# Three-block float32 network on one core: convolutions that read PSUM banks, and three small steps of the delta rule placed elsewhere

## The chip, the cores and the metric

The kernel runs on one core of one Trainium2 chip. The metric is the device time in microseconds (us) of one execution of the whole program. Engines are named as the profile names them: PE is TensorE (matmuls), ACT ScalarE, DVE VectorE, POOL GpSimd, SP SyncE, which here only issues DMAs.

## The reference

512 positions of width 1024, float32, go through two "hybrid" layers and then one further layer (sparse attention, a recurrent unit and a feed-forward part), which the change does not touch. A hybrid layer, cut to what the change touches:

```python
def hybrid_layer(x, ...):
    h = rms_norm(x, norm_g)
    proj = jnp.einsum('btd,de->bte', h, w_in)
    (qa, ka, va, za, ba, aa, ub, zb, qc, kc, vc, zc, iq, ik, iw, gates) = split_columns(proj)
    ya = deltanet_branch(qa, ka, va, za, ba, aa, conv_w, a_log, dt_bias, dn_onorm)
    ...
    merged = jnp.sum(gate * projected, axis=2).astype(w_out.dtype)
    return x + jnp.einsum('btd,de->bte', merged, w_out).astype(x.dtype)

def deltanet_branch(qa, ka, va, za, ba, aa, conv_w, a_log, dt_bias, o_norm):
    qkv = jax.nn.silu(causal_depthwise_conv(jnp.concatenate([qa, ka, va], axis=-1), conv_w))
    q, k, v = jnp.split(qkv, 3, axis=-1)
    q = l2_normalize(q.reshape(b, t, DN_HEADS, DN_DK))
    k = l2_normalize(k.reshape(b, t, DN_HEADS, DN_DK))
    beta = jax.nn.sigmoid(ba.astype(jnp.float32))
    g = -jnp.exp(a_log) * jax.nn.softplus(aa + dt_bias)
    o = chunk_gated_delta_rule(q, k, v, beta, g)
    o = rms_norm(o, o_norm) * jax.nn.silu(za.reshape(b, t, DN_HEADS, DN_DV))
```

The convolution has four taps over time, per channel. There are four heads of width 128 for each of q, k and v, so twelve groups of 128 channels.

## The kernel before

**Products.** Channels lie in the partitions, the 512 positions in the free dimension. Every weight matrix is cut into "units" of 128x1024 values (303 in all, in the fixed order of `plan()`). To get float32 accuracy, weights and inputs are split into a high and a low part, and a product of 128x128 weights with a 128x512 input is three matmuls (`prod3`): high by high, high by low, low by high. A tile of 128 output channels is one unit: eight such products, 24 matmuls, into one PSUM bank. Each unit goes through a ring of three buffers: SP loads it to `st`, ACT rounds it to `wh` (128x1024), POOL computes `wl` = `st` - `wh` (two pieces of 128x512), PE uses it. ACT may round unit u only when PE is done with unit u-3 (`ahead`, called by `take`), SP may load unit u only when POOL is done with u-3.

**Order.** Each engine runs its own program in order; semaphores join them. A main stage is a generator, and side stages are other generators advanced beside it at fixed rates by `weave` (0.81 steps of `delta` per main step in the stage `proj`; a main step is half a tile). What is left of a side when the main stage ends runs after it, with nothing beside it. A layer goes:

- `norm`: the layer's norm and four gate tiles.
- `front1`: the small tile (beta, decay, index weights), then twelve tiles q, k, v of the delta rule, into banks 4 to 7 in turn. Convolution c: ACT copies the bank to `pad[c % 2]` behind three zeros, writes the first tap to `cv` (a `tmp` buffer) with a second read of the bank, and so frees the bank; DVE adds the other three taps from shifted parts of `pad` (each waits for the one before); ACT computes the tanh; DVE multiplies (silu) into `qf`, `kf` or `vf`. `small(1)`, inside convolution 1, computes the decay's softplus in partitions 32 to 35: Abs, Exp, Ln and an Exp of `a_log` on ACT, three DVE instructions, the last a scan into `L.rw`. SP then copies that row (`rows`).
- `proj` beside `delta` and `select`: three index tiles (two queries, one key; each is copied, swapped by DMAs and rotated on DVE), eight rows for attention and twenty gate tiles. `delta` begins with the head norms: ACT squares eight tiles (`dn_sq`), PE sums them over partitions (`sums`, four matmuls each for q and k), ACT takes the reciprocal root (`rnorm`: Ln and Exp), PE spreads it over the partitions (`spread`, four matmuls into banks 4 to 7), DVE multiplies. Then a transpose of `L.rw` (`tp`), sums of the decay (`gl`), products and inverses per chunk, and four chunks in sequence, whose outputs ACT copies to `L.yA`. It ends with the output norm: four squares, `sums`, `rnorm`, `spread`, and four DVE multiplications (`on_row`). `select` chooses the keys by rounds of maxima on DVE.
- `front3` beside `sparse`: four units of values (`v`), gates, pooling. After the selection and `on_row`, SP loads queries, keys and stored gates; `sparse` is the attention.
- the merge and the output projection.

Helpers record the operations, so most lines of the profile are a helper's: L442 is a matmul, L431 a copy on ACT, L428 another activation, L376, L382, L386 DVE or POOL elementwise operations (L386 the multiply-add `scalar_tensor_tensor`), L371 a DMA. Tiles tell the place: `wl<-st,wh` is POOL's split, `tmp<-pad,col,tmp` a convolution tap, `bank<-E,cst` and `bank<-R,cst` the sums and spreads of the norms.

Of the kernel before, what the change touches and what calls it, by code (L numbers as in the profile page):

```python
# [274 lines left out]
class Nothing:  # L275
# [18 lines left out]
    "act_rows": "pl_p qk_sq qk_r q2_sq q2_r k2_sq k2_r conv_th zc_a pl_a ga_a gelu_a rec_a",  # L294
# [215 lines left out]
def build(nc, units, consts, tabA, tabB, cols, poolw, lruw, phi1, phi2, x_in, x_out, cpack, apack, bpack):  # L510
# [9 lines left out]
    def done(*key):  # L520
        return at("unit", place[key])
# [30 lines left out]
    for l in range(2):  # L552
# [20 lines left out]
        L.Y, L.E, L.R = [[sb(f"{n}{e}{l}", [128, T], stack=dtmp) for e in range(2)] for n in "YER"]  # L573
# [154 lines left out]
    def tensor_program(e):  # L728
# [89 lines left out]

        def delta(l):
            L, aa4 = layer[l], layer[l].aa4  # L820
            def sums(b, name, *key):

                o = bank(b, name, *key)
                for c, q in enumerate(Q4):
                    pe.wait_ge(*at(f"{name}_sq", *key, c))
                    t = pe.mm(o[q, :], ones[:, 0:32], (L.aa4k if key[1:] == (1,) else aa4)[c][:], True, True)
                t.then_inc(*sig(f"{name}_mm", *key))

            def spread(src, name, *key):

                pe.wait_ge(*at(f"{name}_r", *key))
                for c, q in enumerate(Q4):
                    t = pe.mm(bank(4 + c, f"{name}_row", *key, c), first[q, :], src[q, :], True, True)
                t.then_inc(*sig(f"{name}_up", *key))

            yield
            sums(4, "dn", l, 0)
            yield
            sums(5, "dn", l, 1)
# [8 lines left out]
            for i in range(4):  # L848
                t = pe.tr(o[:, sq4(i)], L.rw[:, sq4(i)], ident)
# [81 lines left out]
            yield  # L931
            sums(4, "on", l)
            yield
            yield
            spread(aa4[0], "on", l)
            yield

# [16 lines left out]
        def front3(l):  # L954
            L, g = layer[l], f"n{l}"
            for b in range(4):
                bank(b, "vs", l, b)
            for j in range(4):
                n = take("v", l, j)
                for b in range(4):  # L960
                    for kk in range(2):
# [7 lines left out]
                t.then_inc(*sig("unit", n))  # L969
                yield  # L970
# [322 lines left out]
    def scalar_program(e):  # L1293
# [72 lines left out]
        def front1(l):  # L1366
# [4 lines left out]
            z1, z2 = L.E  # L1371

            def small(c):
                if c == 0:
                    ac.wait_ge(*done("small", l))
                    ac.act(L.scs[R0, :], banks[4][R0, :], ACT.Tanh, 0.5).then_inc(*sig("small_a", l, 0))
                if c == 1:
# [76 lines left out]
        def delta(l):  # L1454
# [63 lines left out]
            for c in range(4):  # L1518
                ac.act(aa4[c][:], L.yA[:, c, :], ACT.Square).then_inc(*sig("on_sq", l, c))
# [1492 lines left out]
```

## Time and profile before

| | |
|---|---|
| time, median of 3 runs | 2039.75 us (2035.28 to 2040.04) |
| the profiled execution: its own time | 2041.28 us |
| the profiled execution: span | 2039.5 us |
| PE busy | 1991.6 us (98% of the span), 9420 matmuls |
| PE weight loads busy | 1568.8 us (77%) |
| DVE busy | 1067.9 us (52%) |
| ACT busy | 914.9 us (45%) |
| POOL busy | 874.6 us (43%) |
| DMA | 228.53 MB, mean 112 GB/s |
| mean granted TensorE clock | 0.994 of full speed |

The span is that of one profiled execution, from first to last instruction; the time beside it is the device time of the same execution. Busy shares are means over many stages. A matmul of 128x512 is shown with about 0.39 us, though in an unbroken row the next one begins 0.23 us after it: matmuls overlap, and a busy PE can still be held up for a part of each of these intervals. So the starts of matmuls in the timeline say more than the busy share. Idle time of another engine costs nothing by itself.

### The profile page before, as it was taken

How to read it: one execution, taken by the hardware profiler on the slowest of the kernel's cores; microseconds unless marked ns; L12 is line 12 of the kernel's file. 1: busy time of each engine (PE TensorE's matmuls, PEld its weight loads, DVE VectorE, ACT ScalarE, POOL GpSimd, SP SyncE). 2: the span in 40 equal slices, each digit the busy share in tenths (PEclk: the TensorE clock that was granted, in tenths of full speed). 3: DMA queues.
4: the chain of work that ended last, by engine and by line, in shares of the span. 5: the costliest groups of instructions: out<-in, count | busy, mean ns of one | idle time of the engine just before them, and what ended most of it. 6: DMA issues, size and time to landing. Idle time of an engine off the chain costs nothing.

```text
span 2039.5 us, 24488 instructions
## 1 busy us (share of the span) xinstructions
PE 1991.6 (98%) x9420; PEld 1568.8 (77%) x9420; DVE 1067.9 (52%) x1877; ACT 914.9 (45%) x1414; POOL 874.6 (43%) x646
## 2 busy tenths in 40 slices
PE   8999999999999999999999999999999999999999
PEld 6767778777788768787877788676777887888887
DVE  6756845645746658655464747677344256201210
ACT  5555543334345455443334345677555444312321
POOL 5444432434355445431434455455222345444443
PEclk9999999999999999999999999999999999999999
DMA  5234442323534244532423545322111332332232
GB/s 190 97 114 125 139 134 89 136 83 109 185 107 150 87 122 129 154 104 71 151 79 127 178 155 157 132 71 83 53 52 42 108 105 87 103 98 96 96 111 75
DMA packets 90917, 228.53 MB, mean 112 GB/s; under 512 B 25929, under 2 KB 29001, under 8 KB 89489
## 3 DMA queue, kind: packets, MB, share of 16 engines
q1 hardware_dynamic: 89360, 223.82, 33.4%
q10 hardware_dynamic: 1440, 3.15, 0.4%
q8 instruction: 75, 1.23, 0.2%
q14 instruction: 42, 0.34, 0.1%
HBM read 195.06 MB, written 24.64 MB: 108 GB/s over the span
## 4 chain that ended last, share of the span: by engine, by line
PE 73%; DVE 14%; ACT 6%; DMA 3%; issue 2%; SPq 2%; POOL 1%; ACTq 0%; DVEq 0%
PE bank L442 71%; DVE tmp L386 4%; PE bank L445 2%; SPq L371 2%; ACT tmp L428 1%; ACT wh L431 1%; DVE kv L376 1%; DVE E L376 1%; DVE lt L386 1%; POOL wl L376 1%; DVE tmp L376 1%; DMA gt<-gates 1%; DMA pad<-tmp 1%; ACT pad L431 1%; DVE scs L401 1%
## 5 line engine op out<-in xcount | busy, mean ns | idle before, releaser
L376 POOL TENSOR_TENSOR wl<-st,wh 128x512 fp32r<-128x512 f32 x606 | 826.5, 1386 | 1082.7 <-ACT wh L431 1082.6
L442 PE MATMUL bank<-hh,wh 128*128 128x512 f32 x1632 | 664.5, 407 | 18.8 <-POOL wl L376 15.2
L442 PE MATMUL bank<-hl,wh 128*128 128x512 f32 x1632 | 638.6, 391 | 0.0
L442 PE MATMUL bank<-hh,wl 128*128 128x512 f32 x1632 | 638.6, 391 | 0.0
L431 ACT ACTIVATE wh<-st 128x1024 fp32r<-128x1024 f32 x303 | 318.1, 1050 | 235.6 <-PE bank L442 197.5
L442 PEld LDWEIGHTS bank<-hh,wh 128*128 128x128 f32 x1632 | 307.7, 189 | 122.1 <-issue 28.2
L442 PEld LDWEIGHTS bank<-hl,wh 128*128 128x128 f32 x1632 | 308.0, 189 | 66.9 <-issue 6.9
L442 PEld LDWEIGHTS bank<-hh,wl 128*128 128x128 f32 x1632 | 307.7, 189 | 66.1
L376 DVE TENSOR_TENSOR xt<-xt,bank 128x512 f32<-128x512 f32 x40 | 27.4, 687 | 235.7 <-PE bank L442 235.7
L386 DVE SCALAR_TENSOR_TENSOR tmp<-pad,col,tmp 128x512 f32<-128x512 f32 x80 | 81.7, 1022 | 38.9 <-ACT tmp L428 36.9
L442 PE MATMUL bank<-fh,wh 128*128 128x512 f32 x256 | 99.6, 389 | 0.0
L442 PE MATMUL bank<-fl,wh 128*128 128x512 f32 x256 | 99.6, 389 | 0.0
L442 PE MATMUL bank<-fh,wl 128*128 128x512 f32 x256 | 99.6, 389 | 0.0
L428 ACT ACTIVATE tmp<-bank 128x512 f32<-128x512 f32 x62 | 36.9, 596 | 125.6 <-PE bank L442 118.3
L376 DVE TENSOR_TENSOR tmp<-tmp 128x512 f32<-128x512 f32 x32 | 24.6, 770 | 106.4 <-ACT tmp L428 106.3
L442 PE MATMUL bank<-yh,wh 128*128 128x512 f32 x192 | 79.7, 415 | 0.3 <-DVE yl L376 0.3
L428 ACT ACTIVATE tmp<-bank,hb 128x512 f32<-128x512 f32 x40 | 27.6, 689 | 108.3 <-PE bank L442 94.4
L442 PE MATMUL bank<-yh,wl 128*128 128x512 f32 x192 | 75.0, 391 | 0.0
L442 PE MATMUL bank<-yl,wh 128*128 128x512 f32 x192 | 74.8, 390 | 0.0
L428 ACT ACTIVATE tmp<-tmp 128x512 f32<-128x512 f32 x46 | 29.1, 632 | 74.3 <-DVE tmp L386 73.8
L404 DVE CUSTOM_DVE_ANT_0 Ln<-bank,cau 128x128 f32<-128x128 f32 (+3 forms) x64 | 28.9, 489 | 58.0 <-PE bank L442 57.9
L428 ACT ACTIVATE Ln<-Ln,stc 128x128 f32<-128x128 f32 (+3 forms) x64 | 35.5, 556 | 48.9 <-DVE stc L404 48.8
(340 smaller groups left out, 3000.3 us busy)
## 6 DMA issues: line engine op xcount, KB each, us to landing
st<-units SPq DMA_DIRECT2D x303, 512.0 KB, 3.5
gates<-tmp SPq DMA_DIRECT2D x48, 256.0 KB, 2.5
gt<-gates SPq DMA_DIRECT2D x48, 256.0 KB, 3.7
pad<-tmp SPq DMA_DIRECT2D x32, 128.0 KB, 4.6
qk<-tmp SPq DMA_DIRECT2D x16, 256.0 KB, 4.2
x_scratch<-xt SPq DMA_DIRECT2D x2, 2048.0 KB, 8.6
xt<-x_scratch SPq DMA_DIRECT2D x2, 2048.0 KB, 9.1
ph<-phi SPq DMA_DIRECT2D x8, 512.0 KB, 4.5
```

The source lines that it names most:

```text
L371: return NOTHING if self.e is None else self.e.dma_start(out, in_)
L376: return NOTHING if self.e is None else self.e.tensor_tensor(out, a, b, op)
L386: return NOTHING if self.e is None else self.e.scalar_tensor_tensor(out=out, in0=a, scalar=s, in1=b, op0=op0, op1=op1)
L401: return NOTHING if self.e is None else self.e.match_replace(out, vals, a, v)
L404: return NOTHING if self.e is None else self.e.tensor_tensor_reduce(out, a, b, scale, init, ALU.add, red, acc)
L428: return self.e.activation(out, a, func, scale=scale, **kw)
L431: return NOTHING if self.e is None else self.e.activation(out, a, ACT.Copy)
L442: return NOTHING if self.e is None else self.e.matmul(out, lhsT, rhs, start=start, stop=stop, skip_group_check=share)
L445: return NOTHING if self.e is None else self.e.transpose(out, a, ident)
```

## The change

1. **Convolutions.** ACT no longer copies the bank to `pad`. It writes the first tap; DVE adds taps 1 to 3 from the bank itself, each to the columns from its shift on (511, 510 and 509 columns), and the third of them frees the bank. ACT rounds the next unit (`take`) between its first tap and its tanh, while DVE works.
2. **Softplus of the decay.** Its four activations move from convolution 1 to the step of `delta` behind the two `rnorm` of the head norms, its three DVE instructions to just ahead of DVE's multiplication of k, and the copy of the row on SP to the eighth step of `delta`. Its tiles are `L.Y` and not `L.E`.
3. **Squares of the head norms.** Each is computed in convolution c + 4, behind its tanh. PE's two `sums` stand in one step, with one wait each.
4. **Output norm.** Each chunk of `yA` is squared right behind its copy, into the joined tile `L.ER` (E and R of before). `sums` comes behind the first unit of values, `rnorm` in ACT's second step of values, `spread` behind the third unit, and DVE's four multiplications behind all of the selection. Banks 0 to 3 are taken one by one in the first unit of values.
5. The transpose `tp` takes 96 partitions instead of 128.

The core of the diff:

```diff
@@ PE, front3 @@
+                    if j == 0:
+                        bank(b, "vs", l, b)
...
+                if j == 0:
+                    pe.wait_ge(*at("on_sq", l, 3))
+                    sums(4, L.aa4, "on", l)
+                if j == 2:
+                    spread(L.aa4[0], "on", l)
@@ PE, delta @@
-            sums(4, "dn", l, 0)
-            yield
-            sums(5, "dn", l, 1)
+            pe.wait_ge(*at("dn_sq", l, 0, 3))
+            sums(4, aa4, "dn", l, 0)
+            pe.wait_ge(*at("dn_sq", l, 1, 3))
+            sums(5, L.aa4k, "dn", l, 1)
+            yield
...
-                t = pe.tr(o[:, sq4(i)], L.rw[:, sq4(i)], ident)
+                t = pe.tr(o[:, 128 * i:128 * i + 96], L.rw[0:96, sq4(i)], ident[0:96, 0:96])
@@ ACT, front1 @@
-                ac.cp(pad[c % 2][:, 3:3 + T], banks[b][:])
-                ac.act(cv[:], banks[b][:], ACT.Identity, K(f"conv{l}", 4 * c + 3), 0.0).then_inc(*sig(f"free{b}", "conv", l, c))
-                small(c)
-                ac.wait_ge(*at("conv_v", l, c, 3))
+                ac.act(cv[:], banks[b][:], ACT.Identity, K(f"conv{l}", 4 * c + 3), 0.0).then_inc(*sig("conv_0", l, c))
...
+                if c < 11:
+                    take("p", l, 128 * (c + 1))
+                ac.wait_ge(*at(f"free{b}", "conv", l, c))
                 ac.act(th[:], cv[:], ACT.Tanh, 0.5).then_inc(*sig("conv_th", l, c))
+                if c >= 4:
+                    f, h = c // 4 - 1, c % 4
+                    ac.wait_ge(*at("conv_v", l, c - 4, 4))
+                    ac.act((L.aa4, L.aa4k)[f][h][:], (L.qf, L.kf)[f][:, h, :], ACT.Square, 0.5).then_inc(*sig("dn_sq", l, f, h))
@@ ACT, end of delta @@
+                ac.wait_ge(*at(f"free{5 + n % 2}", "yA", l, n))
+                ac.act(L.ER[:, :, sq4(n)], L.yA[:, :, sq4(n)], ACT.Square).then_inc(*sig("on_sq", l, n))
@@ DVE, front1 @@
-                dv.wait_ge(*at(f"free{b}", "conv", l, c))
+                dv.wait_ge(*at("conv_0", l, c))
                 for i in range(1, 4):
...
-                    dv.stt(cv[:], pad[c % 2][:, 3 - i:3 - i + T], K(f"conv{l}", 4 * c + 3 - i), cv[:], ALU.mult, ALU.add).then_inc(*sig("conv_v", l, c, i))
+                    t = dv.stt(cv[:, i:T], banks[b][:, 0:T - i], K(f"conv{l}", 4 * c + 3 - i), cv[:, i:T], ALU.mult, ALU.add)
@@ SP, delta @@
-            yield from idle(8 + 2)
+            yield from idle(7)
+            sp.wait_ge(*at("small_v", l, 4))
+            sp.dma(L.rw[R3, :], L.rw[R1, :]).then_inc(*dma("rows", l))
+            yield from idle(3)
```

Where instructions move, at the three places that the prediction speaks of:

ACT, one convolution of `front1` (c = 5), before; the pair of rows from bank is the copy and the first tap, the last row the tanh:

```order
L431 ACTIVATE wh<-st 128x1024 [waits s_st0]
L431 ACTIVATE pad<-bank 128x512 [waits s_unit]
L428 ACTIVATE tmp<-bank,col 128x512
L428 ACTIVATE tmp<-tmp 128x512 [waits s_dve_rows]
L431 ACTIVATE wh<-st 128x1024 [waits s_st1]
```

and now (c = 7), where `ER<-qf` is a square of the head norms:

```order
L428 ACTIVATE tmp<-bank,col 128x512 [waits s_dve_rows,s_unit]
L431 ACTIVATE wh<-st 128x1024 [waits s_st0]
L428 ACTIVATE tmp<-tmp 128x512 [waits s_free4]
L428 ACTIVATE ER<-qf 128x512
L428 ACTIVATE tmp<-bank,col 128x512 [waits s_dve_rows,s_unit]
```

The rounding of a unit stood between the tanh and the next first tap; it now stands between the first tap and the tanh.

ACT in the index stage of `proj`, before, from the copy of the second index tile on; each pair `E<-bank,cst`, `E<-E` is one `rnorm`:

```order
L431 ACTIVATE tmp<-bank 128x512 [waits s_unit]
L420 ACT_TABLE_LOAD [waits s_pe_heads]
L428 ACTIVATE E<-bank,cst 128x512
L428 ACTIVATE E<-E 128x512 [waits s_free4]
L431 ACTIVATE wh<-st 128x1024 [waits s_st0]
L428 ACTIVATE E<-bank,cst 128x512 [waits s_pe_heads]
L428 ACTIVATE E<-E 128x512 [waits s_free5]
```

and now, the rows on 4 partitions being the softplus:

```order
L431 ACTIVATE tmp<-bank 128x512 [waits s_unit]
L420 ACT_TABLE_LOAD [waits s_pe_heads]
L428 ACTIVATE ER<-bank,cst 128x512
L428 ACTIVATE ER<-ER 128x512 [waits s_free4]
L428 ACTIVATE ER<-bank,cst 128x512 [waits s_pe_heads]
L428 ACTIVATE ER<-ER 128x512 [waits s_free5]
L428 ACTIVATE Y<-Y 4x512 [waits s_dve_small]
L428 ACTIVATE Y<-Y 4x512 [waits s_act_small] x2
L428 ACTIVATE colx<-col 4x1
L431 ACTIVATE wh<-st 128x1024 [waits s_st0]
```

The rounding of the weights (of gate tile 4) has moved behind the second `rnorm` and the softplus.

PE at the end of `delta`, before, where `ki,qi` is the last product of the selection and `wh,hh` the first of the values:

```order
L442 MATMUL bank<-ki,qi 128x512 [waits s_free3]
L442 MATMUL bank<-E,cst 32x512 [waits s_act_heads] x2
L442 MATMUL bank<-R,cst 32x512 [waits s_act_heads] x2
L442 MATMUL bank<-E,cst 128x512 [waits s_free4,s_act_heads]
L442 MATMUL bank<-E,cst 128x512 [waits s_free5]
L442 MATMUL bank<-E,cst 128x512 [waits s_free6]
L442 MATMUL bank<-E,cst 128x512
L442 MATMUL bank<-wh,hh 128x512 [waits s_free3,s_free2,s_lo,s_free1,s_free0]
```

and now:

```order
L442 MATMUL bank<-ki,qi 128x512 [waits s_free3]
L442 MATMUL bank<-wh,hh 128x512 [waits s_free0,s_lo]
L442 MATMUL bank<-wh,hl 128x512
L442 MATMUL bank<-wl,hh 128x512
```

The values follow the selection's product at once; the four sums stand a unit of 24 matmuls later, the four matmuls of the spread 48 further ones behind them.

## Rows read from the trace of the kernel before

**Rows 1.** Waits of TensorE, whole span: engine, line, waited for; us in total, times, longest.
```profile
PE bank L442 <- POOL wl L376: 18.1, 25, 2.9
PE bank L442 <- ACT E L428: 7.5, 4, 2.7
```

**Rows 2.** Timeline of PE, layer 0, convolution stage: start us, us, operation.
```profile
43.97 0.39 PE L442 MATMUL bank<-hh,wh 128*128 128x512 f32 x1
...
63.01 0.39 PE L442 MATMUL bank<-hh,wh 128*128 128x512 f32 x1
...
65.59 0.50 PE L442 MATMUL bank<-hh,wh 128*128 128x512 f32 x1 [1.74 <-POOL wl L376]
...
120.48 0.50 PE L442 MATMUL bank<-hh,wh 128*128 128x512 f32 x1 [0.28 <-POOL wl L376]
```

**Rows 3.** Timeline of DVE and ACT, one convolution of layer 0.
```profile
70.37 3.28 DVE L386 SCALAR_TENSOR_TENSOR tmp<-pad,col,tmp 128x512 f32<-128x512 f32 x3 [1.32 <-ACT tmp L428]
...
73.69 0.63 ACT L428 ACTIVATE tmp<-tmp 128x512 f32<-128x512 f32 x1 [3.35 <-DVE tmp L386]
74.23 1.04 ACT L431 ACTIVATE wh<-st 128x1024 fp32r<-128x1024 f32 x1
75.18 0.58 ACT L431 ACTIVATE pad<-bank 128x512 f32<-128x512 f32 x1
75.65 0.68 ACT L428 ACTIVATE tmp<-bank,col 128x512 f32<-128x512 f32 x1
```

**Rows 4.** Timeline of PE, layer 0, sums and spread of the head norms.
```profile
126.96 0.50 PE L442 MATMUL bank<-hh,wh 128*128 128x512 f32 x1
...
129.91 1.06 PE L442 MATMUL bank<-aT,cst 128*32 128x512 f32 x8
...
130.90 0.50 PE L442 MATMUL bank<-hh,wh 128*128 128x512 f32 x1
...
135.92 0.50 PE L442 MATMUL bank<-hh,wh 128*128 128x512 f32 x1
```

**Rows 5.** Timeline of PE, layer 1, the same two ends of the stage.
```profile
659.03 0.39 PE L442 MATMUL bank<-hh,wh 128*128 128x512 f32 x1
...
730.90 0.50 PE L442 MATMUL bank<-hh,wh 128*128 128x512 f32 x1
```

**Rows 6.** Timeline of DVE and POOL: multiply-adds that read a bank.
```profile
138.80 2.48 DVE L386 SCALAR_TENSOR_TENSOR qf<-qf,bank 128x512 f32<-128x512 f32 x4
...
360.40 1.60 DVE L386 SCALAR_TENSOR_TENSOR scs<-bank,wi,scs 128x512 f32<-128x512 f32 x2 [3.08 <-ACT bank L428]
...
140.59 2.55 POOL L376 TENSOR_TENSOR wl<-st,wh 128x512 fp32r<-128x512 f32 x2 [3.78 <-ACT wh L431]
```

**Rows 7.** Timeline of PE: end of the delta rule, layer 0, and one product of layer 1.
```profile
358.43 1.52 PE L442 MATMUL bank<-E,cst 128*32 128x512 f32 x4
...
364.78 0.50 PE L442 MATMUL bank<-wh,hh 128*128 128x512 f32 x1
...
963.00 0.63 PE L442 MATMUL bank<-wh,hl 128*128 128x512 f32 x1
```

**Rows 8.** Timelines of ACT, DVE and PE: softplus' steps, and the index stage.
```profile
55.72 1.29 ACT L428 ACTIVATE E<-E 4x512 f32<-4x512 f32 x2
...
61.57 1.21 DVE L395 TENSOR_TENSOR_SCAN rw<-cst,E 4x512 f32<-4x512 f32 x1
...
133.19 1.04 ACT L431 ACTIVATE wh<-st 128x1024 fp32r<-128x1024 f32 x1
...
143.47 0.69 DVE L376 TENSOR_TENSOR ki<-tmp,tabs 128x512 f32<-128x512 f32 x1 [2.19 <-DMA tmp<-tmp]
...
149.09 0.60 PE L445 MATMUL bank<-cst,rw 128*128 128x128 f32 x4
```

**Rows 9.** Timelines of SP and PE: loads after the selection, first product with the loaded keys.
```profile
390.14 0.33 SPq L371 DMA_DIRECT2D pw<-poolw  x1
...
425.66 0.38 PE L442 MATMUL bank<-ks,qs 128*128 128x128 f32 x2
```

More of the change, by code:

```diff
@@ L572, in build @@
         L.XT0 = sb(f"XT0{l}", [128, 4, 4, 128], stack=dtmp)
-        L.Y, L.E, L.R = [[sb(f"{n}{e}{l}", [128, T], stack=dtmp) for e in range(2)] for n in "YER"]
+        L.Y = [sb(f"Y{e}{l}", [128, T], stack=dtmp) for e in range(2)]
+        L.ER = sb(f"ER{l}", [128, 4, T], stack=dtmp)
+        L.E, L.R = [L.ER[:, e, :] for e in range(2)], [L.ER[:, 2 + e, :] for e in range(2)]
         kv = sb(f"kv{l}", [128, 4, T], stack=dtmp)
@@ L817, in proj, with sums, spread @@
             yield from lagged(jobs())
+        def sums(b, x, name, *key):
+            o = bank(b, name, *key)
+            for c, q in enumerate(Q4):
+                t = pe.mm(o[q, :], ones[:, 0:32], x[c][:], True, True)
+            t.then_inc(*sig(f"{name}_mm", *key))
+        def spread(src, name, *key):
+            pe.wait_ge(*at(f"{name}_r", *key))
+            for c, q in enumerate(Q4):
+                t = pe.mm(bank(4 + c, f"{name}_row", *key, c), first[q, :], src[q, :], True, True)
+            t.then_inc(*sig(f"{name}_up", *key))
         def delta(l):
             L, aa4 = layer[l], layer[l].aa4
[L821 to L834, printed above, removed]
             yield
-            sums(4, "dn", l, 0)
+            pe.wait_ge(*at("dn_sq", l, 0, 3))
+            sums(4, aa4, "dn", l, 0)
+            pe.wait_ge(*at("dn_sq", l, 1, 3))
+            sums(5, L.aa4k, "dn", l, 1)
             yield
-            sums(5, "dn", l, 1)
             yield
@@ L1456, in delta @@
             ac.wait_ge(*at("hb2", l))
-            for f in range(2):
-                for c in range(4):
-                    ac.wait_ge(*at("conv_v", l, 4 * f + c, 4))
-                    ac.act((aa4, L.aa4k)[f][c][:], (L.qf, L.kf)[f][:, c, :], ACT.Square, 0.5).then_inc(*sig("dn_sq", l, f, c))
-                yield
+            yield
+            yield
             for f in range(2):
@@ L2170, in delta @@
                 yield
-            yield
-            yield
-            yield
-            dv.wait_ge(*at("on_up", l))
-            dv.wait_ge(*at("hn", l))
-            for c in range(4):
-                dv.stt(L.yA[:, c, :], L.yA[:, c, :], colx[:, 1:2], banks[4 + c][:], ALU.mult, ALU.mult).then_inc(*sig(f"free{4 + c}", "on_row", l, c))
-            yield
         def select(l):
@@ L2219, in front3 @@
             L = layer[l]
-            yield from idle(4)
+            yield from idle(3)
+            dv.wait_ge(*at("on_up", l))
+            dv.wait_ge(*at("hn", l))
+            for c in range(4):
+                dv.stt(L.yA[:, c, :], L.yA[:, c, :], colx[:, 1:2], banks[4 + c][:], ALU.mult, ALU.mult).then_inc(*sig(f"free{4 + c}", "on_row", l, c))
+            yield
             for c in range(4):
@@ L2791, in delta @@
             L = layer[l]
-            yield from idle(8 + 2)
+            yield from idle(7)
+            sp.wait_ge(*at("small_v", l, 4))
+            sp.dma(L.rw[R3, :], L.rw[R1, :]).then_inc(*dma("rows", l))
+            yield from idle(3)
             for f in range(2):
```

82 lines of the change are left out of this document (29 added, 53 removed).

## The prediction, made before the changed kernel ran

> **What bounds the kernel now.** I read the busy table first: PE is busy for 1991.6 of 2039.5 us. The other engines are near half, so only time in which PE stands still, or works slower than it can, is to be won. The list of PE's waits says where [rows 1]: the largest are 18.1 us in 25 waits for POOL's low halves of weights, and 7.5 us in 4 waits for ACT's work on tile E, which are the squares and roots of the norms. These are the two places that the change works on. The timelines give their true size, since a modelled matmul covers part of a gap.
>
> In an unbroken row of tiles the k-steps of three matmuls begin 0.68 us apart: 28 steps lie between 43.97 and 63.01 [rows 2]. A tile of eight takes 5.44 us. From the fourth convolution on a tile takes longer: the one that could begin at 63.69 (63.01 + 0.68) begins at 65.59, and nine tiles later, at 120.48, PE has spent 54.9 us, 6.1 each.
>
> The loop that sets this is one convolution [rows 3]. DVE's three taps run from 70.37 for 3.28 us, the tanh begins at 73.69, the rounding of a unit at 74.23, the copy to `pad` at 75.18, the first tap at 75.65, and the next three taps can begin at about 76.37: 6.0 us round, all in series. The rounding of weights sits in it, so POOL and PE go at this pace.
>
> **Part 1, convolutions, softplus and squares: the stage up to the head norms' first spread.** The new loop from the end of a tile: first tap 0.62, three taps, tanh 0.63, for c from 4 a square of 0.6, and about 0.15 of handovers. The rounding lies beside the taps. No row shows this bank-reading tap. The nearest from below are four independent bank-reading multiply-adds in 2.48 us, 0.62 each; from above two dependent ones in 1.60, 0.80 each [rows 6]; the present taps take 3.28 / 3 = 1.09 [rows 3]. I take 0.80, since the taps depend on each other too: 2.4 us. The loop is 4.4 us, with 1.09 it would be 5.3. Both are below 5.44, so PE runs its tiles unbroken. ACT rounds at about 0.7 us after a tile's end, POOL needs some 2.6 [rows 6], the unit is needed 10.9 after it: ample.
>
> The present taps are slow beside POOL, and the bank-reading ones are not: in rows 6, DVE's run from 138.80 and POOL's split from 140.59 overlap, and both keep their pace. The Trainium skill, "SBUF — State Buffer", Who interferes with whom, says that a DVE instruction with two SBUF inputs and a GpSimd one that reads SBUF block each other, one with a single SBUF input does not. By that rule the trace agrees; without it the loop would be 5.3 and the sum the same.
>
> Now the sum, layer 0. Today from 63.69 to the first matmul behind the spread, 135.92 [rows 4]: 72.2 us. Afterwards: nine tiles 49.0; half a tile 2.7; two `sums` of 1.0 (129.91 to 130.90) make 2.0; half a tile behind an insertion 2.95 (126.96 to 129.91). That is 56.6 to the end of the second index tile. From this point the spread ends today at 135.92 - 129.91 = 6.0, of which 1.0 is the second `sums`; I keep 5.1, since ACT's table load and first root remain. Together 61.7, so **10.5 us less**. Squares are ready: that of k's last head ends some 4.4 us behind the last convolution's tile, PE wants it at 8.2. Layer 1 today: 659.03 + 0.68 = 659.7 to 730.90, 71.2 [rows 5], so **9.5 us less**.
>
> **Part 2, output norm.** The selection's last product hands over at 358.43 and the values begin at 364.78 [rows 7], 6.35 us, which hold four sums, a wait of 2.7 for the root [rows 1], and the spread. Afterwards the matmuls remain, beside the values: 1.0 for the sums, 1.1 for the spread, and 0.23 each for breaking the row (2.95 - 2.72, rows 4), so 2.5 in all. The root has two units, 10.9 us, to be ready and takes under 3. **3.85 less per layer, 7.7 in both.** The squares by chunk leave one square of 0.6 before the selection's work, where there were four.
>
> DVE's four multiplications come behind all rounds of maxima, and SP's loads behind them. Now these start at 390.14 and the keys are first used at 425.66 [rows 9]. The loads end up some 2.4 us later against PE than now, with over 20 in hand. I cost it at nothing; without that cover it would be 2.4 a layer.
>
> **Part 3, what the moved softplus delays.** It leaves the loop, but enters the index stage. Counted from the end of the second index tile (129.91 now), ACT rounds gate tile 4's weights at 3.3 (133.19) [rows 8]; now a second root (two activations, 1.3) and the softplus (two in 1.29 [rows 8], a third, a small one: 2.4) go first, so 3.7 later. SP's queue loads a unit only behind that unit's low half, and the DMAs that swap the index keys stand behind this load. Today the low half is done at 133.19 + 1.05 + 2.55 = 136.8 while the swaps wait for the third index tile's copy anyway, until about 139.5: 2.4 us with the load in between are spare, 1.3 remain. DVE's index keys, now at 143.47 (13.6), come at 14.9, take 2.0, then come softplus' three instructions (1.21 for the scan [rows 8], about 2.4 in all) and the first multiplication of k, 0.7: bank 4 is free at 20.0. PE wants it for the transpose at 149.09 (19.2), less the 0.9 that part 1 took between: 18.3. That is a **new wait of 1.7**, and 0.5 for the next step `gl`, behind four multiplications, row 0 and three small copies: 2.2 a layer, 4.4 in both. From below the bound is 0 (DVE's and SP's queues make up the 2.4 of softplus), from above twice as much, 8.8. SP's copy of the decay's row is queued behind a gate's store and lands some 2 us before PE needs it: nothing. Fewer table loads, the narrower transpose and the missing copies to `pad` are off PE's path: nothing, too.
>
> **Sum.** 10.5 + 9.5 + 7.7 - 4.4 = 23.3 us less. The profiled execution's 2041.28 would become 2018.0. It stood 1.5 above the median of the runs; from the median, 2039.75, I get **2016.4 us**.
>
> **The clock.** At 963.00 a matmul of layer 1 takes 0.63 and the next begins 0.43 after it [rows 7]: the lower level, 1.2 GHz, for eight matmuls, behind the wait for the root. Against 0.23 that costs 1.6 us. The same wait in layer 0 shows none. Such a stretch may vanish here, or appear behind one of the new waits. I leave it out of the sum, but it is 1.6 down and, once a layer, 3.2 up in the range.
>
> **Rivals.**
> A. *No new wait.* DVE and SP absorb the softplus. 4.4 less than my sum: 2012. For it: DVE is idle between index tiles. Against: the order puts it between two things that PE waits for. Chance 0.22.
> B. *The index stage costs double,* because the delayed rounding also holds a unit, or a slow stretch follows: 4.4 to 8 above my sum, 2021 to 2024. Chance 0.15.
> C. *The gain is passed on and lost.* PE comes earlier everywhere, and the chain of inverses or the attention's loads were next to end: the time stays within 6 us of today's, 2037. Against: between the stage and these chains the same steps follow at the same distances, and the lists show waits of only a few us there. Chance 0.05.
> D. *Slower: bank reads with a high price.* If each dependent tap from a bank took as long as a DVE instruction that is held up by POOL, 3.28 - 2 x 0.8 = 1.7, the loop would be 0.62 + 5.1 + 0.63 + 0.6 + 0.15 = 7.1. Twelve of them take 85 us against 65 for the tiles, less the 5 that the ring gives: 15 a layer, where about 9 are lost today. With 7.7 won and 4.4 lost elsewhere: 2 x 6 - 7.7 + 4.4 = 8.7 more, **2048**. It decides once a tap costs over about 1.4 us. Against it stand the 0.80 and the undisturbed overlap of rows 6. The Trainium skill, "VectorE: DVE Perf Modes", Rules for kernel authors, speaks against the change: many operations on a matmul's output should be preceded by a copy to SBUF. In rows 3 and 6 the copied operand was no faster. Chance 0.03.
>
> **The numbers.** My forecast has 0.55, A 0.22, B 0.15, C 0.05, D 0.03. The runs before spread by 2.5 us around their middle, and 0.3% (6 us) is what a measurement can tell from none. The range takes A, with a vanished slow stretch and that spread, 2012 - 1.6 - 2.4 = 2008, and B's end, 2024; C and D are outside. Faster by over 0.3%: forecast, A and B, 0.92; same: C, 0.05; slower: D, 0.03.
>
> **What would show it.** PE's timeline in the convolution stage: tiles 5.44 apart, no wait for POOL's `wl` between convolution 3 and the sums; the sum of such waits falls from 18.1 to about 9. Waits for E (now ER) fall from 7.5 to about 1. Bank-reading taps 0.75 to 0.85 apart, the three within 2.6, also beside POOL. The values' first matmul directly behind the selection's product, without the root's wait. A new wait of 1 to 3 us at the transpose of `rw` or at `gl` behind DVE's `kf`; if there is none, A. If tiles are still over 5.5 apart, the loop is mis-sized and part 1 falls. If waits at the inverses' DMAs grow by more than 3, C.

## The result and the profile after

The changed kernel takes 2022.79 us (median of 4 runs, 2021.52 to 2023.39), the kernel before, run beside it, 2039.03 (2035.28 to 2040.04): ratio 0.9923, 95% interval 0.9906 to 0.994, so 16.2 us faster. The profiled execution took 2022.96 us with a span of 2021.2, 18.3 less than the span before. The forecast was 2016.4, in a range of 2008 to 2024: the time lies inside the range, 6.4 us above the forecast itself.

The list of TensorE's waits of the changed kernel, with the same columns as [rows 1]:

```profile
PE bank L442 <- POOL wl L376: 10.5, 6, 2.9
PE bank L445 <- DVE kf L386: 9.7, 2, 5.0
PE bank L442 <- DMA XT<-inverses: 5.8, 2, 3.0
...
PE bank L442 <- ACT ER L428: 1.3, 2, 0.6
```

The waits for POOL's low halves fell from 18.1 us in 25 to 10.5 in 6, those for the norms' tile from 7.5 to 1.3: the two places that were to be cleared are clear. But there is a new line, 9.7 us in two waits for DVE's multiplication of k. The transpose of `rw` now waits 4.7 and 5.0 us, one wait in each layer, where the forecast had 1.7. And the waits for the inverses' DMAs went from 3.1 to 5.8.

**The convolution stage.** The timelines of DVE, ACT and POOL of the changed kernel, one convolution of layer 0, the counterpart of [rows 3]:

```profile
103.79 0.69 ACT L428 ACTIVATE tmp<-bank,col 128x512 f32<-128x512 f32 x1 [1.21 <-PE bank L442]
104.37 1.05 ACT L431 ACTIVATE wh<-st 128x1024 fp32r<-128x1024 f32 x1
106.86 0.63 ACT L428 ACTIVATE tmp<-tmp 128x512 f32<-128x512 f32 x1 [1.44 <-DVE tmp L386]
...
104.51 2.32 DVE L386 SCALAR_TENSOR_TENSOR tmp<-bank,col,tmp 128x511 f32<-128x511 f32 x3 [1.35 <-ACT tmp L428]
...
105.50 2.54 POOL L376 TENSOR_TENSOR wl<-st,wh 128x512 fp32r<-128x512 f32 x2 [2.89 <-ACT wh L431]
```

Three taps take 2.32 us, 0.77 each, although POOL's split runs from 105.50 beside two of them. ACT now waits for PE's bank (1.21), not PE for ACT: the loop has slack. The next first tap is at 109.23, 5.44 after 103.79, which is PE's own pace.

PE's timeline of the changed kernel, layer 0, from the stage to the transpose, the counterpart of [rows 4], and the transpose of layer 1:

```profile
63.47 0.39 PE L442 MATMUL bank<-hh,wh 128*128 128x512 f32 x1
...
116.51 0.39 PE L442 MATMUL bank<-hh,wh 128*128 128x512 f32 x1
...
117.28 1.06 PE L442 MATMUL bank<-ER,cst 128*32 128x512 f32 x8
...
125.54 1.71 PE L442 MATMUL bank<-ER,cst 32*128 32x512 f32 x8 [0.63 <-ACT ER L428]
...
145.24 0.90 PE L445 MATMUL bank<-cst,rw 96*128 96x96 f32 x4 [4.72 <-DVE kf L386]
...
146.42 0.63 PE L442 MATMUL bank<-hl,wh 128*128 128x512 f32 x1
...
734.96 0.90 PE L445 MATMUL bank<-cst,rw 96*128 96x96 f32 x4 [5.00 <-DVE kf L386]
```

From 63.47 to 116.51 lie 78 k-steps, 53.04 us: 0.68 each, without a break. The spread comes at 125.54, where it was at 133.85 before. Behind the wait of 4.72 the matmuls last 0.63, not 0.39. In layer 1 the spread of this kernel stands at 714.96.

**The index stage,** where that wait comes from: the timelines of ACT, POOL, SP and DVE of the changed kernel, layer 0.

```profile
126.75 1.95 ACT L428 ACTIVATE Y<-Y 4x512 f32<-4x512 f32 x3
...
128.82 1.07 ACT L431 ACTIVATE wh<-st 128x1024 fp32r<-128x1024 f32 x1
...
129.96 5.32 POOL L376 TENSOR_TENSOR wl<-st,wh 128x512 fp32r<-128x512 f32 x4 [6.94 <-ACT wh L431]
137.97 3.41 POOL L376 TENSOR_TENSOR wl<-st,wh 128x512 fp32r<-128x512 f32 x2 [2.69 <-ACT wh L431]
...
132.81 0.33 SPq L371 DMA_DIRECT2D st<-units  x1
133.18 2.41 SPq L371 DMA_DIRECT2D tmp<-tmp  x4
...
137.86 0.69 DVE L376 TENSOR_TENSOR ki<-tmp,tabs 128x512 f32<-128x512 f32 x1 [5.11 <-DMA tmp<-tmp]
138.47 1.78 DVE L376 TENSOR_TENSOR tmp<-tmp,tabs 128x512 f32<-128x512 f32 x1
140.29 1.64 DVE L376 TENSOR_TENSOR ki<-ki,tmp 128x512 f32<-128x512 f32 x1
...
143.25 1.21 DVE L395 TENSOR_TENSOR_SCAN rw<-cst,Y 4x512 f32<-4x512 f32 x1
144.50 2.48 DVE L386 SCALAR_TENSOR_TENSOR kf<-kf,bank 128x512 f32<-128x512 f32 x4
```

The softplus ends on ACT at 128.8, the gate's rounding follows, POOL's low half is done at 132.6, and only then SP loads a unit (132.81) and swaps the index keys (133.18). DVE stood idle for 5.11 us until they landed. Its keys then ran beside POOL's next split and two of their three instructions took 1.78 and 1.64, the first 0.69; that split took 3.41 for the usual 2.54. Layer 1 shows the same: keys from 727.55 on, with 1.70, 1.75 and 0.69. Only after that come the softplus' three instructions and the product with k that frees bank 4.

**The values.** PE's timeline of the changed kernel, layer 0, the counterpart of [rows 7]:

```profile
356.38 1.53 PE L442 MATMUL bank<-ki,qi 64*128 64x512 f32 x4
357.85 0.50 PE L442 MATMUL bank<-wh,hh 128*128 128x512 f32 x1
...
363.55 1.06 PE L442 MATMUL bank<-ER,cst 128*32 128x512 f32 x8
...
375.66 1.14 PE L442 MATMUL bank<-ER,cst 32*128 32x512 f32 x8
```

The values begin 1.5 us after the selection's last product begins (356.38 and 357.85), and neither sums nor spread wait.

**Where the time went,** from the starts of the same matmuls in both traces (after less before, us). The head norms' first spread begins at 125.54 for 133.85 before, 8.3 earlier although the stage began 1.85 late, and so on:

| stretch | layer 0 | layer 1 | forecast, each |
|---|---|---|---|
| convolution stage to the start of the spread | -10.2 | -9.5 | -10.5, -9.5 |
| spread to the transpose of `rw` | +4.5 | +4.7 | +2.2 |
| to the next norm product (`nr`) | +2.0 | +2.4 | 0 |
| to the inverses' product | +1.3 | 0 | 0 |
| to the output projection's first `yh` product | -3.8 | -8.2 | -3.85 |

Besides, layer 0 starts its stage 1.85 late (42.95 against 41.10), and 3.3 are gained after layer 1's `yh`. The late start has nothing to do with the change, since the part ahead of the stage is the same work in every kernel here. It is a stretch at the lower clock, in the profile of the changed kernel and not in that of before:

```profile
10.00:13.00 3.00, 3.00 (x9) 2.35 (x8) 2.88 (x3) 3.00 (x7) 2.69 (x2) 0.50 1.04 408
```

This line is a stretch of the span: busy us (count) of PE, its weight loads, DVE, ACT and POOL, then the granted clock (0.50 here, 1.00 in the same stretch before), the DMA share and GB/s. Every profile here whose stage starts near 43 us has such a stretch, none that starts near 41 has one. Single profiles therefore differ by up to 2 us for no reason in the kernel.

Of the 8.2 in layer 1, 3.85 are the output norm; the rest are two stretches of slow matmuls of before that are gone, one at 963.00 [rows 7], one behind the inverses' wait at 861.40. The kernel before had a third one in layer 0, at 249.90, that is gone too: the 1.3 in the table are a new wait of 2.75 for the inverses, less 1.4 for this stretch. And the 3.3 at the end are a wait of 1.4 for DVE before (at 1168.96) and one more slow stretch before (from 1417.25), neither of which is there now; two others before, from 1362.42 and 1393.17, had been taken up by the next waits. All of it adds up to -18.3.

### The profile page after: what moved, and what is told of

Its sections match the earlier page's. It is cut to its first block, busy times and chain, and to the rows that moved or that the text cites. A ratio compares the mean times of both kernels' runs of the same rounds, so it can differ in the third digit from the quotient of the medians.

```text
span 2021.2 us, 24478 instructions
## 1 busy us (share of the span) xinstructions
PE 1974.4 (98%) x9420; PEld 1564.2 (77%) x9420; DVE 1060.2 (52%) x1877; ACT 901.9 (45%) x1386; POOL 870.1 (43%) x646
## 4 chain that ended last, share of the span: by engine, by line
PE 81%; DVE 9%; ACT 3%; DMA 2%; POOL 2%; SPq 1%; issue 1%; ACTq 0%; DVEq 0%
PE bank L442 79%; PE bank L445 2%; SPq L371 1%; DVE ER L376 1%; DVE kv L376 1%; POOL wl L376 1%; DVE lt L386 1%; DVE tmp L376 1%; DVE tmp L386 1%; DVE nacc L386 1%; DVE scs L401 1%; ACT L420 1%; DMA kv<-blocks 1%; ACT lt L428 1%; DVE m8s L398 0%
## 5 line engine op out<-in xcount | busy, mean ns | idle before, releaser
L428 ACT ACTIVATE tmp<-bank 128x512 f32<-128x512 f32 x62 | 36.9, 596 | 119.3 <-PE bank L442 112.1
L386 DVE SCALAR_TENSOR_TENSOR tmp<-bank,col,tmp 128x511 f32<-128x511 f32 (+2 forms) x72 | 53.9, 749 | 37.3 <-ACT tmp L428 35.6
L431 ACT ACTIVATE tmp<-bank 128x512 f32<-128x512 f32 x38 | 22.5, 593 | 79.0 <-PE bank L442 79.0
L428 ACT ACTIVATE Ln<-Ln,stc 128x128 f32<-128x128 f32 (+3 forms) x64 | 35.5, 556 | 48.3 <-DVE stc L404 48.2
```

Of the source, the lines that this page charges most:

```text
L386: return NOTHING if self.e is None else self.e.scalar_tensor_tensor(out=out, in0=a, scalar=s, in1=b, op0=op0, op1=op1)
L428: return self.e.activation(out, a, func, scale=scale, **kw)
L431: return NOTHING if self.e is None else self.e.activation(out, a, ACT.Copy)
```

## Experiments

Each kernel is the changed kernel with one edit, or two where the text says so. Beside the experiments the kernel before took 2036.45 to 2038.03 us in the median, beside the changed kernel 2039.03: a difference between an experiment and the changed kernel is uncertain by some 2 us. Theory from here on: the 4.5 and 4.7 at the transpose are the softplus' work in ACT's, SP's and DVE's queues, in series; the 2.0 and 2.4 behind it are matmuls at the lower clock. Rival: PE simply came earlier, and the loss would show at some wait whatever the softplus does.

### Softplus back in convolution 1

```diff
@@ ACT, front1 @@
                 if c < 11:
                     take("p", l, 128 * (c + 1))
+                if c == 1:
+                    z1, z2 = L.Y
+                    ac.wait_ge(*at("small_v", l, 1))
+                    ac.act(z2[R1, :], z1[R1, :], ACT.Abs).then_inc(*sig("small_a", l, 1))
...
@@ ACT, delta; DVE and SP likewise @@
-            ac.act(z2[R1, :], z1[R1, :], ACT.Abs).then_inc(*sig("small_a", l, 1))
...
```

> The changed kernel (median 2022.8 us) with the softplus of the decay back in convolution 1 (ACT, DVE and the row's copy on SP); all else as changed. Theory (the changed kernel gives back at the transpose of the decay's rows, because the softplus lengthens the chain index keys, softplus, k's multiplication): the two waits of 4.7 and 5.0 us on DVE's kf vanish and so do the stretches at the lower clock behind them (about 1.9 each), against 0 to 1.5 us a layer in the convolution stage: 2010 to 2013 us. Rival (the chain of the chunks' inverses ends next, so PE's earlier arrival is taken back there): waits at the inverses' DMAs, now 2.8 and 3.0, grow by what is won: 2018 to 2022 us.

Measured: 2008.99 us (2005.22 to 2010.43), ratio to before 0.9852, interval 0.9834 to 0.987. PE's transpose in layer 0 of this kernel; that of layer 1, at 721.34, reads the same:

```profile
138.53 0.50 PE L445 MATMUL bank<-cst,rw 96*128 96x96 f32 x4
```

No wait, and the matmuls behind them run at the full pace. 13.8 less than the changed kernel, a little more than expected (2010 to 2013): the table's 9.2 at the transpose and 4.4 behind it are 13.6. In the profiles, spread to `nr` is 6.95 and 7.6 shorter than in the changed kernel, 14.6 in all, while the convolution stage stays the same; its profile also lacks the slow stretch at 10 us (1.8), and has two in the last layer that the changed kernel has not. The whole loss at and behind the transpose belongs to the place of the softplus, and the rival falls. What is passed on is small: waits for the inverses are 4.0 in all.

### DVE's share earlier, ACT's share later, both

The three DVE instructions directly behind the multiplication of q, that is ahead of the index keys:

```diff
-                if f == 1:
+                yield
+                dv.wait_ge(*at("dn_up", l, f))
+                for c in range(4):
+                    x = (L.qf, L.kf)[f][:, c, :]
...
+                if f == 0:
                     z1, z2 = L.Y
```

> The changed kernel with only DVE's three softplus instructions moved, from ahead of k's multiplication to directly behind q's, where DVE now idles 5.1 us for the swapped index keys. Theory: 2.5 us less on the chain to the transpose in each layer, the waits there fall to 2.2 and 2.5, and a stretch at the lower clock may go: 2014 to 2018 us. Rival (inverses end next): 2020 to 2023 us.

Measured: 2017.06 (2016.75 to 2018.3), ratio 0.9896 (0.988 to 0.9911). 5.7 less than the changed kernel; waits at the transpose 1.67 and 2.24.

The four activations one step later, behind the gate tile's rounding:

```diff
+            yield
             z1, z2 = L.Y
             ac.wait_ge(*at("small_v", l, 1))
...
-            yield from idle(5)
+            yield from idle(4)
```

> The changed kernel with only ACT's four softplus instructions one step later, so that the rounding of gate tile 4's weights comes ahead of them. Theory: the load and the key's swaps behind it on SP start about 2.1 us earlier, and DVE's two-input instructions on the keys (now 1.78 and 1.64 us, beside POOL's split) come before that split and take 0.69 each: the wait at the transpose falls by 3 to 4 us a layer: 2011 to 2016 us. If only the order counts and not the overlap with POOL: 2.1 a layer, 2016 to 2019 us. Rival (inverses): 2020 to 2023 us.

Measured: 2011.65 (2011.5 to 2015.77), ratio 0.9873 (0.9855 to 0.9891). 11.1 less; waits 2.71 and 1.99. The keys, 3.75 earlier in layer 0 (134.11), took 0.69, 0.68 and 0.69, as expected, but now the softplus' first two instructions met POOL's split and took 1.80 and 1.30 in layer 0. So the waits fell by 2.0 and 3.0, for an expected 3 to 4.

Both of these edits in one kernel:

> Both of the two moves before in one kernel. Theory: no wait at the transpose, no stretch at the lower clock there: 2009 to 2013 us, at or below the one with the softplus back in convolution 1. Rival (inverses): 2018 to 2022 us.

Measured: 2008.52 (2007.5 to 2009.46), ratio 0.9851 (0.9833 to 0.9869), half a us under the expected 2009 to 2013, no wait at the transpose. The timeline of DVE in this kernel, layer 0:

```profile
133.22 0.68 DVE L386 SCALAR_TENSOR_TENSOR Y<-Y 4x512 f32<-4x512 f32 x1
...
134.52 1.21 DVE L395 TENSOR_TENSOR_SCAN rw<-cst,Y 4x512 f32<-4x512 f32 x1
135.76 0.69 DVE L376 TENSOR_TENSOR ki<-tmp,tabs 128x512 f32<-128x512 f32 x1
...
138.68 2.47 DVE L386 SCALAR_TENSOR_TENSOR kf<-kf,bank 128x512 f32<-128x512 f32 x4
```

The softplus fills the time in which DVE waited for the swaps, and the keys follow it at 135.76 without a wait. The two halves save 5.7 and 11.1 alone, but 14.3 together: once the wait is gone there is nothing left to win. The softplus in the index stage is free if it stands in the gaps, as free as in convolution 1.

### SP: swaps ahead of the unit load

```diff
                 swap(tmp[3], tmp[2], 32, "swap2", l)
+                take()
                 yield
...
-                yield tile(), index_k()
+                yield idle(1), index_k()
```

> The changed kernel, except that SP issues the four DMAs that swap the index keys ahead of the unit load that stands before them, not behind it (in both layers). In the changed kernel the copy of the third index tile ended at 130.84, the load was issued at 132.81 behind POOL's low half, the swaps from 133.18 on, and DVE's index keys began at 137.86. Theory (the softplus on ACT delays the rounding, this delays POOL's low half, this the load, and this the swaps; and the keys' instructions then meet POOL's next piece): the swaps are issued from 130.9 on, the keys begin about 2.3 earlier, at 135.6 on that time axis, beside at most the end of POOL's split of 129.96 to 135.28, their two slow instructions of 1.78 and 1.64 take 0.7 each, so bank 4 is free about 4.3 earlier and the wait at the transpose falls from 4.7 and 5.0 to under 1. Time 2012 to 2017: 4 to 4.5 a layer, and up to 1.9 a layer more if the stretch at the lower clock behind the wait goes too (2009 to 2013). Rival (the keys are late for another reason, the DMAs' own time or DVE's queue, or the softplus' three instructions carry the whole wait): the wait stays at 3 or more, time 2018 to 2023.

Measured: 2013.82 (2009.79 to 2015.93), ratio 0.988 (0.986 to 0.9901). The timelines of SP, POOL, DVE and PE of this kernel, layer 0, and PE's transpose in layer 1:

```profile
130.97 2.41 SPq L371 DMA_DIRECT2D tmp<-tmp  x4
...
130.07 5.06 POOL L376 TENSOR_TENSOR wl<-st,wh 128x512 fp32r<-128x512 f32 x4 [6.95 <-ACT wh L431]
138.07 3.52 POOL L376 TENSOR_TENSOR wl<-st,wh 128x512 fp32r<-128x512 f32 x2 [2.94 <-ACT wh L431]
...
134.81 0.87 DVE L376 TENSOR_TENSOR ki<-tmp,tabs 128x512 f32<-128x512 f32 x1 [2.21 <-DMA tmp<-tmp]
135.60 0.68 DVE L376 TENSOR_TENSOR tmp<-tmp,tabs 128x512 f32<-128x512 f32 x1
...
138.33 2.19 DVE L395 TENSOR_TENSOR_SCAN rw<-cst,Y 4x512 f32<-4x512 f32 x1
...
141.30 0.55 PE L445 MATMUL bank<-cst,rw 96*128 96x96 f32 x4 [0.68 <-DVE kf L386]
...
725.94 0.55 PE L445 MATMUL bank<-cst,rw 96*128 96x96 f32 x4 [2.06 <-DVE kf L386]
```

Two steps of SP's program, exchanged, give 9.0 of the 13.8 us, inside the expected 2012 to 2017. ACT and DVE do the same work in the same order as in the changed kernel: so it is SP's queue that carried ACT's delay over to DVE. The keys came 3.05 earlier and missed POOL's split: 2.2 because the swaps were issued earlier, 0.8 because they took 3.8 us from issue to the keys, not 4.7 as in the changed kernel. The scan met the split instead and took 2.19 for 1.21. In layer 1 the scaling of the decay (1.33 for 0.48) and the scan (2.17) met it, and the wait stayed at 2.06, where I had expected under 1.

### Output norm back at the end of the delta rule

Sums, root, spread and multiplications where they were before; the squares stay with the chunks. PE's part of what is taken out; it goes back into `delta`, and ACT's and DVE's parts likewise:

```diff
@@ PE, front3 @@
-                if j == 0:
-                    pe.wait_ge(*at("on_sq", l, 3))
-                    sums(4, L.aa4, "on", l)
-                if j == 2:
-                    spread(L.aa4[0], "on", l)
```

> The changed kernel with the output norm (sums, root, spread, DVE's multiplications) back at the end of the delta rule; its squares stay by chunk. Theory: 3.85 us a layer come back, less what the squares by chunk save (up to 1 us, since the sums no longer wait for four squares), and 1.6 where the lower clock follows the root's wait: 2028 to 2033 us. Rival (the output norm was hidden by the selection's rounds on DVE anyway): 2022 to 2025 us.

Measured: 2030.69 (2025.66 to 2031.48), ratio 0.9964 (0.9951 to 0.9976): 7.9 more than the changed kernel, and in the expected 2028 to 2033. In the profiles, the stretch from the inverses' product to `yh` is 4.0 longer than in the changed kernel in layer 0 and 5.3 in layer 1, where eight matmuls behind the norm ran at the lower clock; 1.5 come back at the wait for the inverses of layer 1. PE's timeline of this kernel shows the wait for the root:

```profile
361.54 2.09 PE L442 MATMUL bank<-ER,cst 32*128 32x512 f32 x8 [2.83 <-ACT ER L428]
```

The rival (hidden by the selection's rounds, 2022 to 2025) falls.

### The convolution edit, taken apart

Taps from `pad` again, with the rounding left between first tap and tanh:

```diff
+                ac.cp(pad[c % 2][:, 3:3 + T], banks[b][:])
                 ac.act(cv[:], banks[b][:], ACT.Identity, K(f"conv{l}", 4 * c + 3), 0.0)
...
-                    t = dv.stt(cv[:, i:T], banks[b][:, 0:T - i], ...)
+                    dv.stt(cv[:], pad[c % 2][:, 3 - i:3 - i + T], ...)
```

> The changed kernel with the copy to pad back and DVE's taps read from pad; the rounding stays between first tap and tanh. Theory (any loop under 5.44 us will do): the loop is 0.48 + 0.59 + 3.3 + 0.63 + 0.15 = 5.15 without and 5.75 with a square; eight convolutions at 0.3 over the pace of the tiles are held by the ring of three buffers: 2022 to 2026 us. Rival (reading the banks is what frees the stage): the stage's loss comes back, 2031 to 2040 us.

Measured: 2018.97 (2016.34 to 2021.22), ratio 0.991 (0.9896 to 0.9924). My expectation of 2022 to 2026 was wrong, and the rival's 2031 to 2040 was further off. Timelines of DVE, POOL and ACT of this kernel, one convolution:

```profile
102.59 3.24 DVE L386 SCALAR_TENSOR_TENSOR tmp<-pad,col,tmp 128x512 f32<-128x512 f32 x3 [0.58 <-ACT tmp L428]
...
103.58 3.40 POOL L376 TENSOR_TENSOR wl<-st,wh 128x512 fp32r<-128x512 f32 x2 [2.12 <-ACT wh L431]
...
100.34 0.63 ACT L428 ACTIVATE tmp<-tmp 128x512 f32<-128x512 f32 x1 [2.36 <-DVE tmp L386]
105.86 0.63 ACT L428 ACTIVATE tmp<-tmp 128x512 f32<-128x512 f32 x1 [2.36 <-DVE tmp L386]
```

The taps are as slow as in [rows 3], 1.08 each, and slow POOL's split from 2.54 to 3.40, but the round with a square is 5.52 us, not the 5.75 of my sum: 0.08 over PE's pace, 0.6 us in eight convolutions, which the ring of units takes up. No wait appears in the stage. This kernel is even 3.8 faster than the changed one, and its stage is not: from the start to the spread it takes 82.6 in both. The gain lies behind it. In layer 0 a wait of 1.65 for `qf` at the second spread stands in place of the one at the transpose, with that spread and five matmuls behind it slow; in layer 1 the transpose waits 2.50 and no slow matmuls follow; and PE never waits for the inverses' DMAs. Why these came out so I did not test.

Bank reads, with the rounding behind the tanh as before:

```diff
-                if c < 11:
-                    take("p", l, 128 * (c + 1))
                 ac.wait_ge(*at(f"free{b}", "conv", l, c))
                 ac.act(th[:], cv[:], ACT.Tanh, 0.5).then_inc(*sig("conv_th", l, c))
+                if c < 11:
+                    take("p", l, 128 * (c + 1))
```

> The changed kernel with the rounding back behind the tanh; the taps read the banks. Theory (any loop under 5.44 us will do): the loop is 0.62 + 2.3 + 0.63 + 0.95 + 0.6 + 0.15 = 5.25 at most: 2022 to 2024 us. Rival (the rounding's place is what frees the stage): 2031 to 2040 us.

Measured: 2020.31 (2019.44 to 2022.81), ratio 0.9918 (0.9905 to 0.9932), under the expected 2022 to 2024, and far from the rival's 2031. Tiles stay 5.44 apart, without a wait for POOL, and the waits at the transpose are 4.09 and 5.00. Its profile lacks the slow stretch at 10 us, which accounts for 1.9 between the two profiles. Both edits undone together:

> Both undone: taps from pad and the rounding behind the tanh; squares still between the convolutions, the rest as changed. Theory: the loop is 6.0, from the fifth convolution on 6.6 with its square; twelve take 77 us against 65 for the tiles, about 7 us a layer are lost after the ring's slack: 2033 to 2041 us. Rival (the squares are hidden): the loss of the kernel before without its wait for squares, 2032 to 2034 us, with tiles 6.0 apart throughout.

Measured: 2036.28 (2032.91 to 2037.86, 11 runs), ratio 0.9989 (0.998 to 0.9998), 13.5 more than the changed kernel. PE's timeline and its list of waits in this kernel:

```profile
65.02 0.50 PE L442 MATMUL bank<-hh,wh 128*128 128x512 f32 x1 [0.67 <-POOL wl L376]
...
71.03 0.50 PE L442 MATMUL bank<-hh,wh 128*128 128x512 f32 x1 [0.28 <-POOL wl L376]
...
114.32 0.50 PE L442 MATMUL bank<-hh,wh 128*128 128x512 f32 x1 [0.60 <-POOL wl L376]
...
120.68 0.50 PE L442 MATMUL bank<-hh,wh 128*128 128x512 f32 x1 [0.62 <-POOL wl L376]
```

```profile
PE bank L442 <- POOL wl L376: 19.6, 23, 2.9
```

The time lies in the expected 2033 to 2041. Tiles are 6.01 apart in the first convolutions, as before the change, and 6.35 from the fifth on (120.68 - 114.32), where each round holds a square as well; 23 waits for POOL are back. So the squares are not hidden in this loop, as the rival (6.0 throughout) had it, and cost 0.34 a tile, half of my 0.6. The stage to the start of the spread, us:

| | before | changed | taps from `pad` | rounding late | both undone |
|---|---|---|---|---|---|
| layer 0, from the stage's start | 92.8 | 82.6 | 82.6 | 82.6 | 90.3 |
| layer 1, from `yh` of layer 0 | 242.0 | 232.4 | 232.4 | 233.0 | 239.8 |

Undoing both gives back 7.7 and 7.3, 15.1 of the stage's 19.7 us: these need one of the two, either bank reads, or the rounding beside the taps. With either of them alone the round is at or just over 5.44, and the other one buys only slack. The remaining 4.6 go with what this kernel keeps of the change, the squares and `sums` moved and the softplus out of the loop; I did not take them apart. That the time rises by 13.5 and not by 15.1 fits the index stage, where the waits at the transpose are gone and two of 1.6 for `qf`, with slow matmuls behind them, stand in their place.

## Why the prediction was right or wrong

**Part 1** held: -10.2 and -9.5 to the start of the spread. To the matmul behind it, as I had counted (127.18 and 716.60), it is -10.6 and -9.9, for -10.5 and -9.5. Taps of 0.77 for my 0.80, no slowing beside POOL, tiles 5.44 apart, spread ending 5.0 behind the second index tile for my 5.1. What I had as one cause was two, though. I credited the shorter loop to bank reads and rounding together; each suffices.

**Part 2** held: -3.8 in layer 0, for 3.85, and 7.9 for both when undone, for 7.7; that the second number agrees so well is luck in part, since it holds a slow stretch of about 1.4 and 1.5 given back at the inverses. The multiplications behind the selection cost nothing: SP's loads start at 389.61 and the keys are used at 421.29, 31.7 later, where there were 35.5 [rows 9]: 3.8 less in hand, for 2.4 forecast, and no wait.

**Part 3** is the term that failed: "a new wait of 1.7, and 0.5 for the next step" was 4.7 and 5.0 at the transpose and none at `gl`, 9.2 us of PE's time for 4.4, and 4.4 more in matmuls at the lower clock behind it. Its mechanism was right, its size was not. Step by step, counted from the end of the second index tile (122.17 now): rounding at 6.65, forecast 7.0; keys at 15.7, forecast 14.9; bank 4 free at 23.0, forecast 20.0; PE there at 18.3, as forecast. The swaps were issued at 11.0, forecast 10.9, but took 4.7 us until the keys ran, not 3.9. So 0.8 came from the swaps, why is not shown (with the unit load behind them they took 3.8), and 2.1 from two of the keys' instructions, which I had as "take 2.0" for three. I had the rule for this and [rows 6] for the bank-reading ones, and did not apply it to the other side: a chain that moves by 4 us meets other neighbours. The run with SP's two steps exchanged tests this: with the keys off POOL's split they took 0.87, 0.68 and 0.69, and the waits fell to 0.68 and 2.06. It also issues the swaps 2.2 earlier, so it does not measure the overlap alone; the durations do.

The Trainium skill, "SBUF — State Buffer", Who interferes with whom, says of a DVE instruction with two SBUF inputs and a GpSimd one that reads SBUF that they contend, and the traces here agree on both: 1.78 and 1.64 for 0.69, and 3.41 for 2.54.

**The clock** was left out of the sum and given 1.6 to 3.2 in the range. It came, once a layer, behind the new wait. The changed kernel's stretches of layer 0, ahead of the transpose and behind it, with the columns explained above:

```profile
136.00:144.00 8.00, 4.52 (x22) 2.55 (x14) 5.93 (x6) 4.46 (x6) 3.41 (x2) 0.93 0.56 176
145.30:149.40 4.10, 4.10 (x12) 3.34 (x13) 4.07 (x10) 0.00 (x0) 0.00 (x0) 0.50 0.00 0
```

The second one ran at 0.50 of full speed, 1.2 GHz. 16 matmuls in both layers last 0.63 and start 0.43 apart, not 0.23: 3.2, with the transposes themselves and the matmul behind each 4.4. It was paid for by two such stretches of before that vanished, 4.4 in layer 1. Nor was the one at 963.00 the only one of before, as I had read: the profile also shows 0.50 to 0.58 at 249.90, behind the wait at 861.40, and three times in the last layer (from 1362.42, 1393.17 and 1417.25). The profiles gain 18.3 for the 23.3 forecast, 5.0 less. What cost more than in the sum: 4.8 in part 3's waits, 4.4 in the clock behind them, 1.3 at the inverses, 1.85 at the start, 0.3 in the stage, 12.7 together. What the sum did not hold and came off all the same: 4.4 in layer 1 and 3.3 in the last layer, 7.7. That the forecast is off by 5 to 6 and not by more is luck to that extent.

**The rivals.** A (no new wait, 2012) is what the kernels with the softplus elsewhere are: 2008.5 to 2009.0, less than its sum; the first of them has no slow stretch in either layer, while the kernel before has three. B (the stage costs double because a unit is held, or a slow stretch follows, 2021 to 2024) is what happened, and it is B's end of the range that holds the time. Its second reason came true, 2.0 and 2.4 at the lower clock. Its first did not: no unit was held, and the doubled wait was DVE beside POOL and the later swaps. C is seen as a trace of itself: a wait of 2.75 for the inverses is new in layer 0, 1.3 net of a slow stretch that is gone. D is refuted by the 0.77.

**A better version.** With the softplus in convolution 1, or split as in the third of those runs, the time is 2009.0 or 2008.5, 14 us below the changed kernel and 29 below the kernel before. These two are one within their spread.

## What to carry to other kernels

When work is moved off one loop, write down for every queue it enters (here ACT, DVE and SP) what stands behind it and who is idle there: the same softplus cost 13.8 us or nothing measurable, by which side of a rounding and of a wait for a DMA it stood on. A DMA issue that stands behind a wait for a buffer hands one engine's delay to another; exchanging it with its neighbour gave 9.0 us with no work changed. And before crediting a gain to an edit with two parts, undo each part alone: here either sufficed.

## What the runs showed of the hardware

DVE instructions were slowed beside POOL's split by the place of their inputs. With the moving inputs in SBUF: multiplications and additions of two SBUF tiles 1.64 to 1.78 us for 0.69, taps from `pad` 1.08 for 0.77 (the first three of the kernel before, at 50.70, ran with no split beside them and took 2.32 together), the scan 2.19 for 1.21 (but 1.21 also in the kernel before, at 61.57, where the split overlapped 0.76 of it), the silu product 1.07 for 0.69. With one input in a bank: 0.77 a tap, and 0.62 in `qf` and `kf`, the same beside POOL and alone (in the changed kernel `qf` at 130.28 lay wholly beside a split, `kf` at 144.50 beside none; both took 2.48 for four). Slowed too was one that I had not expected, the scaling of the decay, which has one SBUF tile and a column. DVE's timeline of the run with the swaps first, layer 1, and POOL's beside it:

```profile
721.64 1.33 DVE L383 TENSOR_SCALAR Y<-Y,colx 4x512 f32<-4x512 f32 x1
...
720.94 3.16 POOL L376 TENSOR_TENSOR wl<-st,wh 128x512 fp32r<-128x512 f32 x2 [2.03 <-ACT wh L431]
```

It took 1.33 for the 0.48 that it takes alone. The Trainium skill, same page and section, says that `tensor_scalar` can take both port pairs in its fast modes and then contends with GpSimd; this row agrees.

The copy to SBUF that the Trainium skill, "VectorE: DVE Perf Modes", Rules for kernel authors, offers, as one of two choices, for many operations on a matmul's output did not pay here: beside POOL a tap from the bank took 0.77, one from the copy 1.08, and with no split beside it the copy's 0.77 was no faster than the bank's.

TensorE's clock fell behind some waits at the transpose and not behind others, and the length alone does not tell which. Waits in us, all kernels, and the number of matmuls of 0.63 behind each:

| | lower clock followed | none |
|---|---|---|
| wait (matmuls) | 5.00 (9), 5.00 (4), 4.72 (7), 4.61 (9), 4.43 (7), 4.09 (10), 2.71 (4), 2.24 (7), 2.06 (7) | 2.50, 1.99, 1.67, 0.68, and where there was no wait |

At other places waits of the same size did otherwise. At the second spread, 1.65 (taps from `pad`), 1.63 and 1.64 (both undone) were each followed by the lower clock. Ahead of the stretch at 10 us, the same matmul, the first that reads `hl`, waited 1.96 to 2.45 in the five kernels in which the clock then fell, and 1.30, 1.79, 2.27, 2.58, 2.75 and 3.03 in those in which it did not. What decides it stays open.
